# Making the input tables and lag rows of a state-space layer during the last three experts of the layer before it

## The reference, cut to what matters

```python
# block 1, its last step: 16 experts, 64 positions each
xin = h[bidx, idx]                                   # gather
g = einsum('becd,edf->becf', xin, w_gate)            # 1024 -> 2048
u = einsum('becd,edf->becf', xin, w_up)
eo = einsum('becf,efd->becd', silu(g) * u, w_down)   # 2048 -> 1024
out = zeros(...).at[bidx, idx].add(gate * eo)        # scatter

# block 2, its state-space layer: 32 groups of 16 channels, 64 states each
ab  = exp(lam * dt)                                  # complex, one for each state
bb  = (ab - 1) / lam * (b_re + i b_im)               # input matrix
h_t = ab * h_(t-1) + bb @ u_t
y_t = real(c @ h_t) + d_skip * u_t
```

## Time and profile before

| | |
|---|---|
| median of 3 runs | 1469.31 us (1469.21 to 1470.55) |
| the profiled execution | 1469.46 us, of which the span from first to last instruction is 1467.6 us |
| TensorE busy | 1374.2 us, 94% |
| VectorE / ScalarE / POOL busy | 37% / 23% / 8% |
| moved by DMA | 467.31 MB, mean 318 GB/s |
| experts | from about 160 to 1067 us |
| block 2 | from about 1067 us to the end |

### The profile page before, as it was taken

One profiled execution on the slowest core, in us unless ns is written; L12 is line 12 of the kernel. 1 busy time (PEld: TensorE's weight loads), 2 busy tenths in 40 slices (PEclk: granted clock), 3 DMA queues, 4 the chain that ended last, 5 costly groups with the idle time before them and its releaser, 6 DMA issues.

```text
span 1467.6 us, 16657 instructions
## 1 busy us (share of the span) xinstructions
PE 1374.2 (94%) x6713; PEld 737.4 (50%) x6713; DVE 546.7 (37%) x965; ACT 339.7 (23%) x549; POOL 115.3 (8%) x190
## 2 busy tenths in 40 slices
PE   7999999999998898998988988989899999999997
PEld 6778433333333232332332323324378787888876
DVE  7675621121211121121111211213268587756663
ACT  5893110010000000010000000103042465533322
POOL 0000000000000000000000000002022214550000
PEclk9999999999999999999999999999999999999999
DMA  9149899999999999999999999999975133253231
GB/s 324 22 172 385 324 420 406 428 427 428 429 429 430 429 430 430 429 429 429 430 429 429 429 429 428 428 428 428 404 245 139 58 101 86 83 171 134 92 110 58
DMA packets 67827, 467.31 MB, mean 318 GB/s; under 512 B 5760, under 2 KB 30592, under 8 KB 42688
## 3 DMA queue, kind: packets, MB, share of 16 engines
q1 hardware_dynamic: 62864, 454.71, 75.4%
q0 software_dynamic: 4624, 11.44, 3.1%
q10 hardware_dynamic: 288, 0.45, 0.1%
HBM read 458.49 MB, written 7.05 MB: 317 GB/s over the span
## 4 chain that ended last, share of the span: by engine, by line
PE 62%; DMA 30%; DVE 4%; ACT 2%; issue 2%; DVEq 0%; POOL 0%; ACTq 0%
DMA wide<-in_w_up 22%; PE bank L1028 13%; PE bank L970 12%; PE bank L724 8%; PE bank L726 8%; PE bank L725 8%; DMA early<-in_w_up 8%; PE bank L911 4%; PE bank L998 1%; PE bank L1066 1%; DVE nrm L1746 1%; PE bank L1125 1%; PE bank L1153 1%; PE bank L754 1%; PE bank L764 0%
## 5 line engine op out<-in xcount | busy, mean ns | idle before, releaser
L970 PE MATMUL bank<-wide,xinT 128*64 128x512 f32 x1376 | 307.2, 596 | 43.2 <-DMA wide<-in_w_up 24.6
L970 PEld LDWEIGHTS bank<-wide,xinT 128*64 128x64 f32 x1376 | 96.5, 137 | 249.7 <-issue 170.5
L970 PE MATMUL bank<-early,xinT 128*64 128x512 f32 x656 | 147.2, 596 | 19.8 <-DMA early<-in_w_up 11.1
L1746 DVE SCALAR_TENSOR_TENSOR th<-th,bank 128x512 f32<-128x512 f32 x32 | 20.6, 684 | 387.8 <-ACT th L1451 387.8
L1028 PE MATMUL bank<-wide,actT 128*64 128x512 f32 x656 | 145.1, 595 | 3.6 <-issue 3.4
L724 PE MATMUL bank<-hT_lo,ring_r 128*128 128x512 f32 x352 | 138.6, 394 | 1.4 <-ACT gt L1316 1.1
L726 PE MATMUL bank<-hT_hi,ring_r 128*128 128x512 f32 x352 | 137.1, 389 | 0.0
L725 PE MATMUL bank<-hT_hi,ring_r 128*128 128x512 f32 x352 | 137.0, 389 | 0.0
L1451 ACT ACTIVATE th<-bank 128x512 f32<-128x512 f32 x32 | 17.4, 595 | 477.1 <-PE bank L970 477.1
L1743 DVE TENSOR_TENSOR ring_r<-ring,ring_r 128x2048 fp32r<-128x2048 f32 (+1 forms) x40 | 89.4, 2236 | 59.9 <-ACT ring_r L1284 59.4
L970 PEld LDWEIGHTS bank<-early,xinT 128*64 128x64 f32 x656 | 45.9, 137 | 119.2 <-issue 79.1
(11 more groups left out here) (427 smaller groups left out, 1705.4 us busy)
## 6 DMA issues: line engine op xcount, KB each, us to landing
wide<-in_w_gate SPq DMA_DIRECT2D x43, 2048.0 KB, 37.7
wide<-in_w_up SPq DMA_DIRECT2D x42, 2048.0 KB, 39.0
wide<-in_w_down SPq DMA_DIRECT2D x39, 2048.0 KB, 38.5
early<-in_w_down SPq DMA_DIRECT2D x21, 2048.0 KB, 38.5
early<-in_w_up SPq DMA_DIRECT2D x21, 2048.0 KB, 39.0
early<-in_w_gate SPq DMA_DIRECT2D x20, 2048.0 KB, 40.1
ring<-in_w_in SPq DMA_DIRECT2D x25, 1024.0 KB, 6.2
ring<-in_w_out SPq DMA_DIRECT2D x8, 1024.0 KB, 4.9
```

The costliest lines, as they stand in the source:

```text
L970: last = pe.matmul(bank[1 + 2 * (m % 2) + q // 2][o:o + 64, :], xinT[:, k, :], w[:, i, q * 512:(q + 1) * 512], start=(k == 0), stop=(k == ...
L1746: return dve.scalar_tensor_tensor(out_, a, s, b, op0, op1)
```

## The change

Input tables and lag rows of all four parts c are made while the last three experts run (numbers 13, 14 and 15), and are kept in DRAM until block 2 needs them.

- **Areas.** The units of the last three experts cycle through seven areas (`LAST_CYCLE`), the six `wide` ones and one `early` one. The other two are free from the 155th unit after the ring's start, in expert 12 (`TABLES_FREE`), and hold new tiles (`x_...`).
- **Expert 13.** VectorE prepares powers and scaled b (`tables_prepared`) after expert 12's rows are added. ScalarE does two exponentials and two sines for it. POOL loads `x_bc` (512 KB) and makes the first output table for the lags (six operations of 128x512, `output_half`).
- **Expert 14.** After expert 13's rows are added, VectorE makes input tables and lag rows in the order table 0, table 1, lags 0, table 2, lags 1, table 3, lags 2. TensorE does `turned_tables(c)` (8 transposes) after units m = 3, 4, 5, 6 and `table_lags(c)` (16 products) after m = 3, 5, 7. ScalarE copies the transposed table to the single tile `x_st` and sends it to DRAM on its own queue (512 KB), and waits for its landing before the next copy. POOL makes the next output table after each lag product, and stores the lag rows (120 KB) after that.
- **Expert 15.** The last lags: the product after m = 2, the rows after the norms on VectorE, the store on POOL after its powers.
- **Block 2.** `ssm_tables`, `ssm_lags`, `state_rows`, `input_table`, `lag_rows`, the scaling of b and `bbd` are gone. VectorE still prepares the powers, POOL still loads `bc` and makes the output tables. POOL reads the stored tables back (512 KB for each c) into `st_even` and `st_odd`: the first two, one after the other, ahead of output table 0.

```diff
+        LAST_CYCLE = (1, 2, 3, 4, 5, 6, 0)
+            for j in range(TURN * E_UNITS):                         # SP
+                e, m = NE - TURN + j // E_UNITS, j % E_UNITS
+                sp.wait_ge(unit_used, B1_UNITS + last_before(j) + 1)
+                load_expert(e, m, moe_ring[last_slot(j)], moe_full[last_slot(j)], e == LAST and m >= E_UNITS - 2)
...
+            def turned_tables(c):                                   # TensorE
+                pe.wait_ge(wext_ready, c + 1)
+                for i in range(2):
+                    if c:
+                        pe.wait_ge(turned_read, 2 * (c - 1) + i + 1)
+                    for g in range(CGP):
+                        last = pe.transpose(bank[5 + i][:, g * P:(g + 1) * P], x_wext[c % 2][:, i, g, 0:P], ident)
+                    last.then_inc(turned_full, 1)
+            def table_lags(c, b):
+                pe.wait_ge(x_wc_ready, c + 1)
+                if c:
+                    pe.wait_ge(lags_read, c)
...
+                if with_tables:                                     # ahead of expert 14's L998
+                    pe.wait_ge(turned_read, 2 * CT)
+                    pe.wait_ge(lags_read, CT - 1)
...
+            for c in range(CT):                                     # ScalarE, ahead of expert 14
+                if c:
+                    act_e.wait_ge(st_out, 16 * c)
+                for i in range(2):
+                    act_e.wait_ge(turned_full, 2 * c + i + 1)
+                    act_e.activation(x_st[:, i, :], bank[5 + i][:, :], ACT.Copy).then_inc(turned_read, 1)
+                act_e.wait_ge(turned_read, 2 * c + 2)
+                act_e.dma_start(s_dram[c], flat(x_st)).then_inc(st_out, 16)
...
+            lag_output(0)                                           # POOL
+            for c in range(1, CT):
+                lag_output(c)                                       # waits for lags_full c
+                lags_stored(c - 1)                                  # waits for lags_read c
...
+            def lag_rows(c, bk):                                    # VectorE
+                dve.wait_ge(lags_full, c + 1)
+                if c:
+                    dve.wait_ge(l_out, 16 * c)
+            tables_prepared()
+            expert(LAST - 2)
+            input_table(0)
+            for c in range(1, CT):
+                input_table(c)
+                lag_rows(c - 1, 7)
+            expert(LAST - 1, True)
...
-            ssm_tables(0)                                           # TensorE, block 2
-                    ssm_lags(p)
-                    if 0 < c < CT:
-                        ssm_tables(c)
...
+            for c in range(2):                                      # POOL, block 2
+                pool.dma_start(flat(states_of[c].rearrange("p a g c -> p a (g c)")), s_dram[c]).then_inc(st_in, 16)
+                pool.wait_ge(st_in, 16 * (c + 1))
             output_table(0)
```

More of the change, by code:

```diff
@@ L923, in other_rows @@
                                   is_transpose=True, start=(t == 0), stop=False)
+            def turned_tables(c):
[7 more added lines that the diff above has]
+            def table_lags(c, b):
+                pe.wait_ge(bbd_ready, 1)
+                pe.wait_ge(x_wc_ready, c + 1)
+                if c:
+                    pe.wait_ge(lags_read, c)
+                for ri in range(2):
+                    for g in range(CGP):
+                        last = pe.matmul(bank[b][32 * g:32 * g + 32, 0:P], x_bbd[:, ri, c * CGP + g, :], x_wc[:, ri, g, :],
+                                         start=(ri == 0), stop=(ri == 1))
+                last.then_inc(lags_full, 1)
             def gathered_transposes(rows=xg):
@@ L930, in gathered_transposes, with expert @@
                 last.then_inc(bank_full[0], 1)
-            def expert(e, turn, r, final=False):
+            def expert(e, turn, r, late=False):
                 first = turn is None
+                final = late and r == TURN - 1
+                with_tables = late and r == TURN - 2
                 def bank_free(b, n):
@@ L976, in expert @@
                         places()
+                    if with_tables and m >= 3:
+                        if m == 3:
+                            for b in (5, 6, 7):
+                                bank_free(b, 0)
+                        if m < 3 + CT:
+                            turned_tables(m - 3)
+                        if m in (3, 5, 7):
+                            table_lags((m - 3) // 2, 7)
+                    if final and m == 2:
+                        bank_free(0, 0)
+                        table_lags(CT - 1, 0)
                     if final and m == 2:
@@ new lines, in tables_prepared, with per_chan @@
+            def tables_prepared():
+                dve.wait_ge(unit_used, TABLES_FREE)
+                dve.memset(flat(x_prep), 0.0).then_inc(x_prep_in, 1)
+                step_angles(x_prep, x_prep_exp, x_prep_sin, x_prep_in, x_sin_arg)
+                first_power(x_prep, x_pw_re, x_pw_im)
+                input_scale(x_prep, x_pw_re, x_pw_im)
+                dve.wait_ge(x_bc_in, 16)
+                def per_chan(v):
+                    return v.unsqueeze(2).to_broadcast([P, GP, SG])
+                sc = [x_prot[:, i, :, 0:SG] for i in range(2)] + [x_prot[:, i, :, SG:2 * SG] for i in range(2)]
+                cmul((x_bc[:, 0, :, :], x_bc[:, 1, :, :]), (x_bc[:, 0, :, :], x_bc[:, 1, :, :]),
+                     (per_chan(x_prep[:, 13, :]), per_chan(x_prep[:, 15, :])), sc)
+                link(dve.memset(x_bbd.rearrange("p a g c -> p (a g c)"), 0.0))
+                for a in range(2):
+                    q = slice(64 * a, 64 * a + 64)
+                    for ri in range(2):
+                        last = dve.tensor_copy(x_bbd[q, ri, :, a * SG:(a + 1) * SG], x_bc[q, ri, :, :])
+                last.then_inc(bbd_ready, 1)
+                powers(x_prep, x_pw_re, x_pw_im, x_pw_in).then_inc(x_pw_ready, 1)
+                dve.memset(lagsb[:, 0:T8 - 1, :].rearrange("p d c -> p (d c)"), 0.0)
+                link(dve.tensor_reduce(diag, ident.rearrange("p (g c) -> p c g", c=SG), AX, ALU.add))
+                dve.wait_ge(x_pw_ready, 1)
@@ L2163, in _ @@
[L2163 to L2170 removed]
+            step_angles(prep, prep_exp, prep_sin, prep_in, sin_arg)
```

330 lines of the change are left out of this document (176 added, 154 removed).

## The result

The changed kernel takes **1480.26 us** (median of 4 runs, 1479.16 to 1480.92), the kernel before beside it 1469.59. The ratio is 1.0071, with a 95% interval of 1.0056 to 1.0086: slower by 10.7 us. The forecast was 1473.6 with a range of 1469.5 to 1480.0, so the direction was right, the size was more than twice the forecast, and the time lies 0.3 us above the range. The profiled execution took 1480.19 us, its span is 1478.4 (before: 1467.6).

What follows compares the result with a forecast made beforehand. The prediction took DMA bytes, with TensorE close behind, to bound the experts, and TensorE's projections block 2. Experts +9.9 and block 2 -5.8 gave +4.1 us: 1473.6, range 1469.5 to 1480.0.

Steps and rivals of the forecast that it cites:

- What bounds the kernel: Up to expert 15's unit m = 7, DMA bytes, with TensorE's work only a few us behind; in block 2, TensorE's projections.
- fewer areas are free: Last three experts: seven areas of weights cost nothing by themselves, as loads are issued about 29 us ahead.
- the full price for writes: While expert weights stream, a write costs the DMA stream as much as a read of its size.
- 7.3 us for the bytes: Experts: 3.11 MB of new traffic at 428 GB/s takes 7.3 us from the stream of weights.
- TensorE's order comes after the bytes: Expert 15, unit m = 7: TensorE ready at 1055.8, weights landed at 1053.2, so experts end 9.9 us later.
- no new waits for `st`, `toep` or `wc` in block 2: Block 2: new waits for these would have shown the forecast wrong altogether; stored tables had 30 us spare.
- the path to the transposes of L998: Expert 14: lag rows, then input table 3, release these transposes at 1004.7, 13.6 us later than before.
- rival 2: Experts: ScalarE's copies into single x_st wait for landings; +15.9 - 5.8 = +10.1, 1479.6; from landings of about 9 us; chance 0.15.
- block 2, -5.8 counted: Block 2: tables and lag products leaving TensorE's order gain 5.8 us, with 7.2 as the upper end.
- As long as nothing else comes last: Block 2: condition under which what TensorE doesn't do there is gained in full.
- the lag rows' chain: Expert 14: lag product, POOL's table 11.0, landing 8.3, VectorE's lag rows, table 3 at 996.1, transposes at 1004.7.
- Some 13 us earlier: Expert 15, m = 7: TensorE's readiness with a landing of 2.6 us and both engines fast; then bytes alone count, 7.3.

Runs made afterwards that it cites:

- areas6: The kernel before with the ring of the last three experts cut from nine areas to six, nothing else changed: 1470.01 us, ratio 1.0003.
- no_stores: loose without the four stores of the tables (2.1 MB), block 2 reading other numbers put in DRAM earlier: 1468.11 us, ratio 0.9989.
- loose: four_tiles with lag rows stored before POOL's next table, input table 0 an expert earlier, transposes and lag products spread from m = 1: 1472.99 us.
- four_tiles: The changed kernel with four tiles instead of one for the transposed tables, six areas left, ScalarE never waiting for a store's landing: 1473.38 us.
- one_tile_loose: The changed kernel, one tile and seven areas kept, with only the schedule of loose: 1473.10 us, ratio 1.0024.

## Why the prediction was right and wrong

**Right.** What bounds the kernel; that fewer areas are free (areas6); the full price for writes (no_stores: 4.9 us measured, 4.9 counted) and with it 7.3 us for the bytes (loose: the last weights land 7.2 later; the fixed point comes 8.0 later, mostly because a slow unit delays the start on them); that TensorE's order comes after the bytes; no new waits for `st`, `toep` or `wc` in block 2.

**Wrong: which wait comes last.** The step that failed is the path to the transposes of L998. The forecast let input table 3, behind the lag rows, release them at 1004.7, and left the wait of ScalarE for `x_st` to rival 2, with a chance of 0.15 and the condition that a store lands in 9 us or more. The landings were 9.99, 10.22 and 11.07. The wait for `x_st` came last, the transposes began at 1009.45, and the experts took 14.8 us more instead of 9.9. Two rows of before were at hand: `gfb` at 10.9 us for a tile of this very size among the weights, and `gf_half` at 8.3 for 128 KB. Read together they said already that a quarter of the bytes saves only a quarter of the time. I took the 10.9 as the far end because it belonged to another queue. At this size the queue made little difference: 10.5 on POOL's for `x_bc`, 10.2 on ScalarE's. With 10.2 + 1.2 per table rival 2's own sum gives 971.6 + 3 x 11.4 = 1005.8 for the end of ScalarE's copies and, with 2.8, 1008.6 for the transposes. They came at 1009.45. Rival 2 was this case. That its 1479.6 is only 0.6 us from the profiled time is partly luck: it had +15.9 for the experts, 1.1 too much, and -5.8 for block 2, 1.8 too much gain.

**Wrong: block 2, -5.8 counted, -4.0 there.** By c, from the traces (before, after, in us up to the values of that c): c = 0, 122.41 and 122.16, counted 2.0, got 0.25. c = 1, 36.10 and 35.16, counted 0.9, got 0.9. c = 2, 35.18 and 33.72, counted 1.45, got 1.46. c = 3, 35.18 and 33.73, counted 1.45, got 1.45. All of the error is c = 0. "As long as nothing else comes last" was written and then looked at only where TensorE already waited. At c = 0 it doesn't wait in before, but VectorE's rounding of the next weights ends 0.73 us ahead of it. Also for this reason the range was too narrow: its upper end took rival 2 with the full 5.8. With -4.0 that end would have been 1.8 us higher and would have held the result.

**Close by luck: the lag rows' chain.** With four tiles the experts take 10.1 us more, where the forecast had 9.9, but two errors meet in it. The forecast had table 3 at 996.1 and the transposes at 1004.7. four_tiles, where this chain alone decides, has 994.15 and 1005.94. The way to table 3 was shorter: POOL's table 8.7 us (972.13 to 980.87) instead of 11.0, the landing 7.9 instead of 8.3. The way from there was longer: 1005.94 - 994.20 = 11.7 us where 8.65 was counted. For the transposes it shows 1.97 instead of 0.9, for unit m = 7 5.62 instead of 3.65, both after a wait of 7.42 us. That is 3.0 us, with a granted clock of 0.60 from 994.20 to 1001.70 (1.00 in before), which was in no term of the sum. four_tiles' 1473.38 is near to the 1473.6 of the forecast, but it doesn't confirm the sum: its trace, taken at 1475.25, has 10.1 us more up to the fixed point and only 4.3 less behind it.

**The sum as it should have been.** Experts: transposes at 1009.45, plus 51.1 counted, gives m = 7 at 1060.55; it came at 1061.05. 1061.05 - 1045.93 = 15.1, less 0.3 in the tail: 14.8. Block 2: -4.0. Together 10.8.

**Slips in the prediction's sums, without effect.** "Some 13 us earlier" with short landings and fast engines comes to 5.7 + 3.7 + 1.4 = 10.8 from its own terms. The range's upper end is called rival 2's, but is +10.5 where that rival's sum is +10.1. The tail behind m = 7 isn't "without a gap": TensorE waits 0.85 us for VectorE there, in after too.

**Not settled.** Loose and one_tile_loose differ by 0.11 us with the intervals wide open around it, so whether the one tile costs anything there is unknown. Between after and four_tiles the medians differ by 6.9 us and the traces by 4.8; the profiled execution of four_tiles (1475.25) was the slowest of its seven. The three slower ones (1474.22 to 1475.25) have a mean granted clock of 0.995 and the four others (1473.13 to 1473.38) of 0.996 to 0.997, so TensorE's clock may be the difference; no trace of a faster one was taken.

## What to carry to other kernels

Beside a full stream of large loads a small transfer's landing went more by its packets than by its bytes: 5.1 to 6.2 us for 32 packets, 6.2 to 7.9 for the 48 of the lag rows, 8.9 to 12.7 for 144. Don't put such a landing between a tile and its next use unless there is room for it. Before a removed operation is counted as gained, look for the engine that ends just ahead of the one relieved, also where the trace shows no wait. And work moved into an expert costs not only its own time: when it makes TensorE wait for long, the products after the wait can be slower as well.

## What the runs showed of the hardware

**TensorE's clock after a wait.** In before the granted clock is 1.00 throughout these stretches, with waits of up to 1.7 us. In after, the products behind the wait of 6.12 us run in a window with 0.50 granted, the level of 1.2 GHz (window 995.10:999.00 above). In 1013 to 1020, behind the third wait and the transposes, it is 1.00 again. Transposes take 1.94 to 1.97 us instead of 1.09, a unit 4.70 to 5.62 instead of 3.65. So 1.9 us (after) and 3.0 us (four_tiles) more pass behind such a wait. In four_tiles they delay the end; in after the wait of 3.57 us for `x_st` follows and covers them. The transposes after the wait of 2.52 in after are slow as well (1.94). After two waits of the same length it went both ways; the first row is of loose, the second of no_stores:

```profile
989.61 3.65 PE L1035 MATMUL bank<-wide,xinT 128*64 128x512 f32 x16 [2.51 <-DMA wide<-in_w_up]
```
```profile
987.13 5.35 PE L1035 MATMUL bank<-wide,xinT 128*64 128x512 f32 x16 [2.51 <-DMA wide<-in_w_up]
```

What else decides there wasn't tried. In before nothing in the rows of experts 14 and 15 could have shown it, since no wait there is longer than 1.7 us.

**VectorE and POOL are slower side by side.** In after, VectorE's operations on 128x512 of the input tables take 0.68 us alone and 1.43 to 1.76 beside POOL's table, and POOL's 1.04 to 1.27 alone and 1.39 to 1.62 beside VectorE's. These rows are VectorE's timeline of after; POOL's table began at 985.45:

```profile
987.40 0.68 DVE L1839 TENSOR_TENSOR x_wext<-x_pw_re,x_bc 128x512 f32<-128x512 f32 x1
988.00 1.76 DVE L1839 TENSOR_TENSOR x_tmp<-x_pw_im,x_bc 128x512 f32<-128x512 f32 x1
989.79 1.43 DVE L1839 TENSOR_TENSOR x_wext<-x_wext,x_tmp 128x512 f32<-128x512 f32 x1
```

The two rates are those of the earlier trace rows for VectorE (0.68 and 1.55), at a slow end 0.2 higher. The first of the three rows, 0.68, lies beside POOL's work too; why it isn't slower is not explained.
